# Decoder layer in one kernel: the inversion stages begin one slot later and stand closer, the second low-rank product two slots later, the second solve in a slot of its own

## The chip, the cores and the metric

The kernel runs on one core of a Trainium2 chip. The metric is the device time of one execution in microseconds, taken as the median of three runs. The core's engines run in parallel and each takes its own instructions strictly in the order in which they were written: TensorE (PE, with its weight loads PEld) multiplies matrices, VectorE (DVE), ScalarE (ACT) and GpSimd (POOL) work element by element, SyncE (SP) issues the transfers. They wait for each other only through semaphores.

## The reference

One inference step of a decoder layer for 256 prompt rows and 8 sequences of 4 sample rows (NT = 288 columns in the kernel, NX = 296 with the 8 rows before the samples), model width 2048. Cut to what matters:

```
P  = rmsnorm(x) @ w_in                      # 2048 x 14784, the columns of all branches
r, k, v = shifted mixes of P's columns      # z = prw + mu * (prw_prev - prw)
w  = -softplus(-(w0 + tanh(wd) @ w2)) - 0.5 # first low-rank product;  decay = exp(-exp(w))
a  = sigmoid(a0 + ad @ a2)                  # second low-rank product
kk = k * k_kk;  kk = kk * rsqrt(sum(kk * kk over the head))
k  = k * (1 + (a - 1) * k_a)
per head of 64, over the rows in order:
    sa = S @ -kk;  S = S * w + sa x (kk * a) + v x k;  y = S @ r
h  = RG-LRU scan of the causal conv of P's columns (a second branch)
x  = x + (g_a * (h * gelu) @ w_rg_o + g_b * out(y) @ w_rw_o) @ w_o
x  = x + relu(rmsnorm(x) @ w_up)^2 @ w_down
x  = x + sigmoid(rmsnorm(x) @ w_ple_gate) * (p @ w_ple)
```

## The kernel before

All large products are done in units: one unit multiplies 128 columns of a weight matrix (2048 x 128, 1 MB, loaded by SP into `raw`) with the activations. ACT copies `raw` to `wh` (the rounded high part) and DVE forms `wl = raw - wh`; PE then does 3 x 16 matmuls per unit (`xh,wh`, `xl,wh`, `xh,wl`, `unit_part`, all recorded on line 612). There are two `wh`/`wl` buffers and two output banks, so one unit is prepared while the other is multiplied.

The first half of the kernel is a loop over 16 pairs of heads (`step`, passes it = 0 to 15 and a last step with it = 16). Each pass has six units (k, r, v, RG input, RG gate, merge gate), and each unit is cut into 8 parts of 6 matmuls: these are the 48 slots of a pass. After the unit's part in a slot, each of the engines does what two tables written by hand name for that slot:

- `LATE[slot]`: stages of the chain of the pair before (it - 1). The recurrence is done in chunks of 64 rows. For it, triangular matrices are inverted in five levels: `invert1a` to `invert5b`. In `inverta` PE multiplies `am` with `tt` and ACT copies the result to `yy` (two copies, lines 1107 and 1108); in `invertb` PE multiplies `yy` and `tn` both ways and DVE adds the result to `inv` (`tt` and `tn` are its two halves). Then for each chunk c: `r`c (PE, ACT copies to `rs`), `u`c, the solve (PE, DVE copies to `us`), `my`c (PE; DVE forms the next state `mp`).
- `EARLY[slot]`: stages of this pair. `wd`: ACT squares `zk` (the mixed k) to `ksq`, PE multiplies `w2s` with `low`, ACT takes the sigmoid of the result to `sigw`. `ad`: PE multiplies `a2s` with `low` into the same bank, once `sigw` has been read out (`sig_ready`); ACT takes the sigmoid to `siga`, DVE forms `kp`. `kk_sum`: PE sums `ksq` over the head, DVE takes it up as `rn`. `decay`: ACT takes an exponential of `sigw` and a root of `rn`, with a table load before each. `kk`: DVE's reciprocal.

Pass 0 has no LATE stages, the last step (units of the second merge gate) has no EARLY ones. Within a slot each engine's order is fixed. ACT: at the first slot of a unit the eviction of the unit before (`evict`, `gb_evict`), then, at parts 0 and 2 of a unit (`HI_AT`), half of the next unit's `wh` (`hi_half`, L1176), then the LATE stages, then the EARLY ones. DVE: at a unit's first slot the mix of the evicted k, r or v (`shift_mix`; `zk` at slot 8), at parts 3 and 4 (`LO_AT`) half of `wl` (L1658), then LATE, then EARLY. PE: the 6 matmuls, LATE, EARLY.

The first slots of a pass hold for DVE the end of the chain before (`var`, slot 46), `ar`, `bonus`, `rg_decay` and the masks of `pairwise` (slot 5: `both`, `inv`), and then `zk`.

Of the kernel before, what the change touches and what calls it, by code (L numbers as in the profile page):

```python
# [65 lines left out]
def constants():  # L66
# [48 lines left out]
HI_AT, LO_AT = (0, 2), (3, 4)  # L115
EARLY = {
    9: ["wd"],
    10: ["ad"],
    13: ["kk_sum"],
    15: ["decay"],  # L120
    18: ["kk"],
    22: ["cum"],
# [6 lines left out]
    4: ["rg_decay"],  # L129
    5: ["pairwise"],  # L130
    6: ["rg_root"],
    9: ["invert1a"],
    10: ["invert1b", "rg_scan"],
    11: ["state_in"],
    12: ["invert2a"],
    14: ["invert2b"],
    15: ["samp_pair"],
    16: ["invert3a"],
    18: ["invert3b"],
    21: ["samp_inv_a", "invert4a", "samp_inv_b"],  # L140
    22: ["invert4b"],
# [3 lines left out]
    28: ["samp_out", "r0"],  # L145
    30: ["u0"],
    31: ["my0"],
    34: ["r1", "u1"],
    36: ["my1"],
    37: ["r2"],  # L150
    39: ["u2"],
# [1746 lines left out]
```

## Time and profile before

| | |
|---|---|
| median of 3 runs | 2811.33 us (2808.49 to 2817.96) |
| the profiled execution: its own time | 2813.93 us |
| its span | 2812.2 us |
| PE busy | 2698.8 us, 96% |
| DVE busy | 1665.3 us, 59% |
| ACT busy | 1162.7 us, 41% |
| PE's mean granted clock | 0.976 of full |

The page sums busy times over the whole span. The loop over the pairs takes the time up to about 1465 us; behind it come the products without a chain beside them. "Idle" in brackets behind a row is the time that its engine stood still just before it, with what ended it.

### The profile page before, as it was taken

How to read it: one execution, taken by the hardware profiler on the slowest of the kernel's cores; microseconds unless marked ns; L12 is line 12 of the kernel's file. 1: busy time of each engine (PE TensorE's matmuls, PEld its weight loads, DVE VectorE, ACT ScalarE, POOL GpSimd, SP SyncE). 2: the span in 40 equal slices, each digit the busy share in tenths (PEclk: the TensorE clock that was granted, in tenths of full speed). 3: DMA queues.
4: the chain of work that ended last, by engine and by line, in shares of the span. 5: the costliest groups of instructions: out<-in, count | busy, mean ns of one | idle time of the engine just before them, and what ended most of it. 6: DMA issues, size and time to landing. Idle time of an engine off the chain costs nothing.

```text
span 2812.2 us, 57470 instructions
## 1 busy us (share of the span) xinstructions
PE 2698.8 (96%) x22780; PEld 2512.8 (89%) x22780; DVE 1665.3 (59%) x2962; ACT 1162.7 (41%) x1626; POOL 103.9 (4%) x89
## 2 busy tenths in 40 slices
PE   5999999999999999999999999999999999999997
PEld 5988888888888888888889999999999999999996
DVE  5666776666776656776644455655544544545655
ACT  3544455444455434454434333344433433423322
POOL 0000000000000000000000000000000000000000
PEclk8999999999999999999999999999999999999998
DMA  5533333333332333233346776555665565565653
GB/s 153 155 91 87 82 88 90 88 90 86 82 101 77 88 90 93 79 101 79 84 107 186 193 214 181 160 162 165 168 169 156 167 168 158 166 168 159 171 151 93
DMA packets 699658, 361.58 MB, mean 129 GB/s; under 512 B 43905, under 2 KB 698531, under 8 KB 698659
## 3 DMA queue, kind: packets, MB, share of 16 engines
q1 hardware_dynamic: 699598, 360.74, 47.2%
q8 instruction: 42, 0.69, 0.1%
q14 instruction: 18, 0.15, 0.0%
HBM read 346.12 MB, written 14.59 MB: 128 GB/s over the span
## 4 chain that ended last, share of the span: by engine, by line
PE 82%; DVE 10%; ACT 2%; issue 2%; DMA 2%; SPq 0%; DVEq 0%; ACTq 0%
PE bank L612 81%; DVE wl L1658 2%; DVE both L1319 1%; DVE sd L1646 1%; PE bank L640 1%; DVE yc L1322 1%; ACT L1064 1%; DVE ysq L1319 1%; DMA raw<-w_in 1%; DVE wl L1316 0%; DVE inv L1319 0%; DVE nrm L1322 0%; DVE sd L1319 0%; DVE sd L1325 0%; DVE ar L1322 0%
## 5 line engine op out<-in xcount | busy, mean ns | idle before, releaser
L612 PE MATMUL bank<-xh,wh 128*128 128x288 f32 (+1 forms) x3136 | 1012.3, 323 | 16.8 <-DVE xl L1319 9.7
L612 PE MATMUL bank<-xl,wh 128*128 128x288 f32 (+1 forms) x3136 | 941.9, 300 | 0.0
L612 PE MATMUL bank<-xh,wl 128*128 128x288 f32 (+1 forms) x3136 | 940.7, 300 | 0.0
L612 PEld LDWEIGHTS bank<-xh,wh 128*128 128x128 f32 x3136 | 601.7, 192 | 56.0 <-issue 14.2
L612 PEld LDWEIGHTS bank<-xl,wh 128*128 128x128 f32 x3136 | 603.9, 193 | 6.8
L1316 DVE TENSOR_TENSOR wl<-raw,wh 128x2048 fp32r<-128x2048 f32 x206 | 472.1, 2292 | 232.2 <-ACT wh L1008 232.1
L612 PEld LDWEIGHTS bank<-xh,wl 128*128 128x128 f32 x3136 | 603.5, 192 | 0.0
L612 PE MATMUL bank<-sbl,wh 128*128 128x288 f32 x1792 | 535.1, 299 | 0.0
L612 PE MATMUL bank<-sbh,wl 128*128 128x288 f32 x1792 | 532.9, 297 | 0.0
L612 PE MATMUL bank<-sbh,wh 128*128 128x288 f32 x1792 | 529.7, 296 | 1.1 <-DVE wl L1316 1.0
L1008 ACT ACTIVATE wh<-raw 128x2048 fp32r<-128x2048 f32 x206 | 392.5, 1905 | 287.1 <-PE bank L612 272.6
L612 PEld LDWEIGHTS bank<-sbh,wh 128*128 128x128 f32 x1792 | 338.3, 189 | 1.6 <-issue 1.2
L612 PEld LDWEIGHTS bank<-sbl,wh 128*128 128x128 f32 x1792 | 336.9, 188 | 0.0
L612 PEld LDWEIGHTS bank<-sbh,wl 128*128 128x128 f32 x1792 | 336.6, 188 | 0.0
L1658 DVE TENSOR_TENSOR wl<-raw,wh 128x1024 fp32r<-128x1024 f32 x204 | 245.0, 1236 | 5.7 <-ACT wh L1176 4.2
L1176 ACT ACTIVATE wh<-raw 128x1024 fp32r<-128x1024 f32 x204 | 212.5, 1051 | 64.2 <-PE bank L612 63.0
L1625 DVE COPY us<-bank 64x128 f32<-64x128 f32 x64 | 18.5, 289 | 225.2 <-PE bank L612 225.2
L1319 DVE TENSOR_TENSOR inv<-inv,bank 64x512 f32<-64x512 f32 (+1 forms) x160 | 100.8, 630 | 69.4 <-PE bank L612 61.0
L1319 DVE TENSOR_TENSOR rga<-rga,bank 128x288 f32 (+1 forms) x80 | 36.3, 454 | 149.5 <-PE bank L612 149.5
L1271 ACT ACTIVATE tmp<-tmp 128x288 f32<-128x288 f32 x64 | 28.5, 445 | 225.3 <-DVE tmp L1322 225.3
L1131 ACT ACTIVATE rs<-bank 64x128 f32<-64x128 f32 x64 | 17.5, 274 | 175.4 <-PE bank L612 175.4
L612 PE MATMUL bank<-inv,both 64*64 64x64 f32 x1280 | 54.5, 224 | 22.2 <-DVE inv L1319 22.2
(286 smaller groups left out, 2769.2 us busy)
## 6 DMA issues: line engine op xcount, KB each, us to landing
raw<-w_in SPq DMA_DIRECT2D x116, 1024.0 KB, 5.8
raw<-w_up SPq DMA_DIRECT2D x64, 1024.0 KB, 6.3
raw<-w_down SPq DMA_DIRECT2D x64, 1024.0 KB, 5.8
raw<-w_rg_o SPq DMA_DIRECT2D x16, 1024.0 KB, 5.9
raw<-w_rw_o SPq DMA_DIRECT2D x16, 1024.0 KB, 5.9
raw<-w_o SPq DMA_DIRECT2D x16, 1024.0 KB, 5.8
raw<-w_ple_gate SPq DMA_DIRECT2D x16, 1024.0 KB, 6.0
s<-state_rwkv SPq DMA_DIRECT2D x32, 128.0 KB, 3.8
```

Of the source, the lines that this page charges most:

```text
L612: return pe.matmul(out, lhsT, rhs, start=start, stop=stop, skip_group_check=True)
L640: return pe.transpose(out, in_, ident)
L1008: act.activation(wh[slot][:], raw[slot][:], ACT.Copy).then_inc(hi_done, 1)
L1064: act.activation(sigw[:], bank[7][:, 0:NT], ACT.Sigmoid, bias=ptu[:, W0:W0 + 1]).then_inc(sig_ready, 1)
L1176: act.activation(wh[slot][:, k, :], raw[slot][:, k, :], ACT.Copy).then_inc((half_done, hi_done)[part], 1)
L1271: act.activation(tmp[u][:], tmp[u][:], ACT.Square).then_inc(h_sq, 1)
L1316: dve.tensor_tensor(wl[slot][:], raw[slot][:], wh[slot][:].bitcast(F32), ALU.subtract).then_inc(lo_done, 1)
L1319: return dve.tensor_tensor(out, x, y, op)
L1322: return dve.scalar_tensor_tensor(out, x, s, y, op0, op1)
L1625: dve.tensor_copy(us[rc, :], bank[5][rc, 0:P]).then_inc(u_read, 1)
L1646: dve.reciprocal(sd[:], sd[:]).then_inc(ch.sem, ch.one())
L1658: ins = dve.tensor_tensor(wl[slot][:, k, :], raw[slot][:, k, :], wh[slot][:, k, :].bitcast(F32), ALU.subtract)
```

## The change

Only the two tables change. `ad` moves from slot 10 to 12 and `kk_sum` from 13 to 14. The inversion's levels 1 to 3 move: 1a from 9 to 10, 1b from 10 to 11, 2a from 12 to 14, 2b from 14 to 15, 3a from 16 to 17 (3b stays at 18). `state_in` moves from 11 to 12, `samp_pair` from 15 to 16. The solve `u1` moves from slot 34, where it stands behind `r1`, to 35. `wd` stays at slot 9.

```diff
 EARLY = {
     9: ["wd"],
-    10: ["ad"],
-    13: ["kk_sum"],
+    12: ["ad"],
+    14: ["kk_sum"],
     15: ["decay"],
...
 LATE = {
...
-    9: ["invert1a"],
-    10: ["invert1b", "rg_scan"],
-    11: ["state_in"],
-    12: ["invert2a"],
-    14: ["invert2b"],
-    15: ["samp_pair"],
-    16: ["invert3a"],
+    10: ["invert1a", "rg_scan"],
+    11: ["invert1b"],
+    12: ["state_in"],
+    14: ["invert2a"],
+    15: ["invert2b"],
+    16: ["samp_pair"],
+    17: ["invert3a"],
     18: ["invert3b"],
...
-    34: ["r1", "u1"],
+    34: ["r1"],
+    35: ["u1"],
     36: ["my1"],
```

## Rows read from the trace of the kernel before

**Rows 1.** The page's parts 1 and 4: busy times, and the chain that ended last.

```profile
PE 2698.8 (96%) x22780; PEld 2512.8 (89%) x22780; DVE 1665.3 (59%) x2962; ACT 1162.7 (41%) x1626; POOL 103.9 (4%) x89
PE 82%; DVE 10%; ACT 2%; issue 2%; DMA 2%; SPq 0%; DVEq 0%; ACTq 0%
```

**Rows 2.** PE's waits, whole span: releaser, total us, times, longest.

```profile
PE bank L612 <- DVE inv L1319: 22.2, 15, 1.5
PE bank L612 <- ACT sigw L1064: 17.8, 15, 1.2
...
PE bank L612 <- ACT rs L1131: 7.1, 16, 0.5
```

**Rows 3.** Timeline of PE, slots 9 to 11 of pass 13: start, duration.

```profile
1140.26 0.68 PE L612 MATMUL bank<-inv,both 64*64 64x64 f32 x16 [1.48 <-DVE inv L1319]
1140.87 0.75 PE L612 MATMUL bank<-low,w2s 96*128 96x288 f32 x2
1141.24 0.51 PE L612 MATMUL bank<-xh,wh 128*128 128x296 f32 x1
...
1142.36 0.68 PE L612 MATMUL bank<-yy,inv 64*64 64x64 f32 x16
...
1144.74 0.75 PE L612 MATMUL bank<-low,a2s 96*128 96x288 f32 x2 [1.23 <-ACT sigw L1064]
```

**Rows 4.** Timeline of ACT in the same slots.

```profile
1140.98 0.38 ACT L1107 ACTIVATE yy<-bank 64x256 f32<-64x256 f32 x1 [1.67 <-PE bank L612]
1141.37 0.38 ACT L1108 ACTIVATE yy<-bank 64x256 f32<-64x256 f32 x1
1142.33 0.54 ACT L1062 ACTIVATE ksq<-zk,ptu 128x288 f32<-128x288 f32 x1 [0.59 <-DVE zk L1322]
1142.89 1.28 ACT L1064 ACT_TABLE_LOAD   x1
1144.18 0.50 ACT L1064 ACTIVATE sigw<-bank,ptu 128x288 f32<-128x288 f32 x1
1144.58 1.05 ACT L1176 ACTIVATE wh<-raw 128x1024 fp32r<-128x1024 f32 x1
```

**Rows 5.** Timeline of DVE in the same slots.

```profile
1140.04 1.21 DVE L1319 TENSOR_TENSOR both<-ab,cst 128x1024 f32<-128x1024 f32 x1
...
1141.78 0.52 DVE L1322 SCALAR_TENSOR_TENSOR zk<-sd,ptu,ex 128x288 f32<-128x288 f32 x1
```

**Rows 6.** Timeline of PE, slots 34 to 36 and 42 to 43 of that pass.

```profile
1189.48 0.41 PE L612 MATMUL bank<-rs,inv 64*64 64x64 f32 x4 [0.45 <-ACT rs L1131]
1189.83 0.40 PE L612 MATMUL bank<-xh,wh 128*128 128x288 f32 x1
...
1191.61 0.37 PE L612 MATMUL bank<-us,tmb 64*128 64x128 f32 x1
...
1202.34 0.40 PE L612 MATMUL bank<-xh,wh 128*128 128x288 f32 x1
...
1203.34 0.37 PE L612 MATMUL bank<-us,tmb 64*128 64x128 f32 x1
```

**Rows 7.** Windows: stretch, length, busy us of each engine, PEclk (granted clock).

```profile
1045.22:1126.56 81.34, 77.85 (x775) 67.46 (x774) 57.05 (x134) 39.29 (x70) 6.41 (x5) 1.00 0.35 90
1126.56:1210.83 84.27, 80.76 (x776) 69.53 (x774) 57.04 (x134) 39.29 (x70) 6.40 (x5) 0.96 0.33 87
1176.60:1183.40 6.80, 6.80 (x33) 4.95 (x31) 0.00 (x0) 0.95 (x5) 0.00 (x0) 0.50 0.60 160
1395.10:1401.90 6.80, 6.00 (x50) 5.87 (x51) 3.61 (x12) 2.34 (x6) 0.00 (x0) 0.50 0.01 2
1410.80:1414.20 3.40, 0.88 (x29) 0.83 (x30) 0.00 (x0) 2.86 (x5) 0.00 (x0) 1.00 0.00 0
```

**Rows 8.** Timeline of PE, slots 10 and 18 of the last step.

```profile
1395.90 1.12 PE L612 MATMUL bank<-yy,inv 64*64 64x64 f32 x16 [3.08 <-ACT yy L1108]
...
1413.37 0.68 PE L612 MATMUL bank<-yy,inv 64*64 64x64 f32 x16 [2.52 <-ACT yy L1108]
```

## The prediction

> **What bounds the kernel.** I read the page first. PE is busy for 96% of the span and holds 82% of the chain that ended last [rows 1]: every us in which PE stands still or runs slowly is a us of the kernel, and time on DVE or ACT counts only where PE waits for it. Next, PE's waits [rows 2]. Three of them belong to the slots that the change touches. PE waits 15 times for `inv` (22.2 us), in front of `invert1a`: 1.48 us in each of passes 2 to 15 and 1.53 us in the last step, none in pass 1. It waits 15 times for `sigw` (17.8 us), in front of `ad`'s product: 1.23 us a pass, 0.67 in pass 1. And it waits 16 times for `rs` (7.1 us), in front of `u1`: 0.45 us a pass. That is the whole gain that could be had: 47 us, 3.2 us a pass.
>
> Then the timeline of one pass, engine by engine, to see what is late. DVE is behind when slot 9 comes: it has come through the masks of `pairwise`, ends the last of them at 1141.25, and only then mixes `zk`, done at 1142.30 [rows 5]. ACT needs `zk` for `ksq`, starts at 1142.33, and goes on through a table load (1.28 us), `sigw`, and the second half of `wh` [rows 4]. So in slots 9 and 10 ACT's queue hangs on DVE's `zk`, and what stands in it ahead of `ksq` gets done early, what stands behind it late. Before the change the two `yy` copies of `invert1a` stand ahead of `ksq`: done at 1141.75 [rows 4], and `invert1b` finds them ready at 1142.36 [rows 3].
>
> **The change, part by part.** No instruction is added or removed; the sum is of waits and of the clock.
>
> `invert1a` one slot later. PE has ended slot 9 at 1140.26 - 1.48 = 1138.78 [rows 3]. `wd`'s product takes it 0.37 us (1140.87 to 1141.24) and the six matmuls of a slot 1.12 us (1141.24 to 1142.36) [rows 3]. It would be at `invert1a` at 1140.27, just as `inv` is ready. The wait of 1.48 us goes.
>
> `ad` in slot 12. `sigw` is read at 1144.68 [rows 4], and in slot 12 PE comes far behind it. The wait of 1.23 us goes.
>
> `invert1b`: here the wait turns up again, larger. The copies of `invert1a` now stand at slot 10, and `wd` stays at slot 9. On ACT both `ksq` and `sigw` are therefore ahead of the copies, and so is the half of `wh` that ACT does at the start of slot 10. ACT's order becomes `ksq` (1142.33, still tied to `zk`: nothing in front of `zk` on DVE is moved), table load, `sigw`, `wh` until 1144.58 + 1.05 = 1145.63, and then the two copies. They begin 0.1 us before `wh`'s row ends, as `wh` did behind `sigw`, and take 1141.75 - 1140.98 = 0.77 us [rows 4]: `yy` is ready at 1146.30. PE comes to `invert1b` at 1140.27 + 0.61 (`invert1a`, 1140.26 to 1140.87 [rows 3]) + 1.00 (a slot, 1202.34 to 1203.34 [rows 6]) = 1141.88. Counted from the end of its last matmul it stands still some 4.4 us. New wait less old ones: 4.4 - 1.48 - 1.23 = +1.7 us a pass. `wd` and `ad` no longer share a group with an inversion stage but `ad` joins `state_in` and `kk_sum` joins `invert2a`: nine groups of small matmuls in slots 9 to 18 before and after, so no cost there.
>
> What is queued behind. On PE, everything: it is the bound. On DVE, `rg_scan` and half a `wl` now come ahead of `invert1b`'s addition; what hides them is the new wait itself: from `zk` at 1142.30 DVE has until PE has ended `invert1b`, at about 1147.5, 5.2 us. If they took longer, two slots and `state_in` still lie between `invert1b` and `invert2a`, some 3 us of cover. On ACT, `siga` comes after `state_in`'s copies, `decay` with its two table loads later than now, and the eviction of the second unit and `invert3a`'s copies after that. Adding up ACT's queue from 1146.3 on I get `yy` for `invert3b` within 0.1 us of PE's coming to it: no wait, with nothing to spare. If that cover is gone it costs tenths of a us a pass. `wl` of the next units is early enough (`hi_half` is at its place). SP and POOL have no stage in the tables; what SP waits for from the moved stages (`kk_mm` at slot 24, `state_mm` at slot 32) was done long ago in either order, so no transfer moves.
>
> `u1` in slot 35. The wait of 0.45 us goes, because PE does a slot meanwhile. But two slots in one piece take 1.78 us (1189.83 to 1191.61) and two with a group between them 2 x 1.00 [rows 6], so the split costs 0.22. Gain: 0.2 us a pass. DVE does the first half of `wl` in front of `us` now; it begins before PE gets to `u1` and takes 1.2 us, so `us` is there for `my1` a slot later. Bounds of this edit: -0.45 to +0.2.
>
> Together 1.7 - 0.2 = 1.5 us a pass with its clock at full; pass 1, where DVE has no chain behind it, has a new wait of some 2.3 us for its old 0.67, the same difference. 15 passes: +22 us. Pass 0 has no inversion. In the last step there is no `wd`; the copies are behind an eviction that waits for a transfer, and half a `wh` more comes ahead of them (+1.0 us), while PE has one slot more to do meanwhile: 0.
>
> The clock. PE's granted clock is at half (1.2 of 2.4 GHz) in some stretches, and a pass with none takes 81.34 us, one with 6.8 us at half 84.27 [rows 7]: 2.9 us for 6.8, 1.5 for 3.4. In the last step PE waited 1.53 us, did one slot and `invert1a`, waited 3.08 us [rows 8], and its clock was at half from 1395.1, 0.8 us before that wait ended, to 1401.9 [rows 7]. A wait of 2.52 us there left it at 1.00 [rows 7, 8], and so do the two waits of 1.48 and 1.23 in each pass now. The new wait of 4.4 us in one piece is longer than the one that was followed by half clock, so I take it that each of passes 2 to 15 gets such a stretch, beside the one after `samp_out` that it has already. Bounds: 0 if it does not come, 2.9 us for 6.8 in full. Some of it falls on the wait itself, where it costs nothing, and some passes will have 3.4 us only; by the last step (6.0 of 6.8 us not covered, 2.6 us) and a short one partly covered (1.0) I take 2.0 us, nearer to the one with its own row. 14 x 2.0 = +28 us.
>
> Sum: 22 + 28 = +50 us. The profiled execution took 2813.93 us for its span of 2812.2; with the change I expect a span of about 2862. The median of the runs shown is 2.6 us under the profiled execution's own time: 2811.3 + 50 = 2861.
>
> On table loads the Trainium skill ("ScalarE: Activation LUTs", section "What ACT_TABLE_LOAD costs") says that each switch costs the load and about 1.38 us of drain, 2.66 us in all. The trace does not agree: the load ends at 1144.17 and `sigw` starts at 1144.18, and `ksq` had ended 0.02 us before the load [rows 4]. If the drain were there the new wait would be 1.4 us longer, +21 us in 15 passes.
>
> **The rivals.** (a) The new wait comes, but no half clock with it: +22 us, 2833. For it: short waits leave the clock alone [rows 7]. Against it: 3.08 us did not. 12 in 100.
> (b) The new wait is met by slack that I do not see (a table load that ACT does ahead of `zk`, a DVE that gets to `zk` sooner): with the load of 1.28 us taken off, the wait is 3.1 us and the pass gains and loses about nothing, 2811 within 8 us. Against it: the load stands behind `ksq` in all passes. 5 in 100.
> (c) Faster: `yy` is ready when PE comes, and the waits just vanish. Then 2.7 + 0.2 us a pass, 15 passes, -43 us: 2768. The point that decides is `zk`: only were it done by about 1137.9 instead of 1142.3 would ACT be through with its four instructions and the copies by 1141.9, and `both` alone runs until 1141.25 [rows 5]. Rather, a part of it together with no half clock. 3 in 100.
> (d) More is lost: each stretch at half is 6.8 us or longer, or ACT's late `decay` makes a second wait at `invert3b`: +75 us or more, 2886. 8 in 100. The drain named above would give 2882; from the rows I give it 1 in 100 of these 8.
> (e) My forecast: both parts, 72 in 100.
>
> **How the numbers follow.** Forecast 2861. Below I take in (a), 2833, with room for a gain of `u1` in full (15 x 0.25 = 4 us); above, 14 stretches at 2.9 us (+13 us) and some tenths at `invert3b` (+5 us). Range 2829 to 2880. 0.3% (8 us) is about what a measurement of this kernel can tell from no change. Faster by more than that: (c) and a little of (b), 0.04. Within: 0.06. Slower: (a), (d), (e), 0.90.
>
> **What would show it.** In the new profile: no wait of PE for `inv` in passes 1 to 15, none for `sigw` or only the shortest, 15 waits for `yy` (L1108), some 4.4 us each, 60 to 65 us in all; `rs` waits gone but for tenths. ACT's order `ksq`, table load, `sigw`, `wh`, `yy`, `yy`. PEclk of a second half-clock stretch in each pass a few us after `invert1a`, the mean clock from 0.976 down to about 0.95. Passes 3 to 4 us longer than the 81.34 and 84.27 us of now. The prediction is wrong if `yy` comes before 1.6 us behind `sigw`'s row, if `zk` is earlier in the pass, or if a wait of over 4 us leaves the clock at full.

## The result and the profile after

The changed kernel takes 2884.50 us (median of five runs, 2879.75 to 2888.82) against 2811.33 for the kernel before (also of five, not three): 73 us slower, a ratio of 1.0258 with a 95% interval of 1.0245 to 1.0272. The forecast was 2861 with a range up to 2880: the side is right and so are two of its terms, but the loss is half as large again (73 us against 50), because a third term had been put at nothing. The profiled execution is the fastest of the five (2879.75 us, span 2878.0); its span is 65.8 us longer than before.

The page of the changed kernel, parts 1, 2 and 4:

```profile
PE 2743.5 (95%) x22780; PEld 2551.8 (89%) x22780; DVE 1667.9 (58%) x2962; ACT 1160.4 (40%) x1626; POOL 103.9 (4%) x89
PEclk8999999999989989999999999999999999999998
PE 82%; DVE 10%; ACT 3%; issue 2%; DMA 1%; DVEq 0%; SPq 0%; ACTq 0%
```

The same number of instructions, yet PE is busy 45 us longer than in [rows 1]: the same matmuls took longer, and that is the clock (its mean fell from 0.976 to 0.957). The other 21 us of the span are time in which PE stood still. Its waits, whole span:

```profile
PE bank L613 <- ACT yy L1109: 68.6, 16, 4.5
...
PE bank L613 <- ACT ysq L1140: 3.8, 16, 0.2
PE bank L613 <- DVE inv L1320: 3.1, 15, 0.6
```

Of [rows 2] the waits for `sigw` and `rs` are gone and that for `inv` is down from 22.2 to 3.1 us. In their place stands one for `yy`. It is 4.46 or 4.47 us in each of passes 2 to 15, 2.28 in pass 1, 3.80 in the last step. Pass 12, PE, the counterpart of [rows 3]:

```profile
1106.85 0.68 PE L613 MATMUL bank<-inv,both 64*64 64x64 f32 x16 [0.20 <-DVE inv L1320]
1107.46 0.41 PE L613 MATMUL bank<-xh,wh 128*128 128x296 f32 x1
...
1113.02 1.12 PE L613 MATMUL bank<-yy,inv 64*64 64x64 f32 x16 [4.46 <-ACT yy L1109]
```

ACT and DVE in the same slots, the counterparts of [rows 4] and [rows 5]:

```profile
1108.93 0.54 ACT L1063 ACTIVATE ksq<-zk,ptu 128x288 f32<-128x288 f32 x1 [3.03 <-DVE zk L1323]
1109.48 1.28 ACT L1065 ACT_TABLE_LOAD   x1
1110.78 0.50 ACT L1065 ACTIVATE sigw<-bank,ptu 128x288 f32<-128x288 f32 x1
1111.17 1.05 ACT L1177 ACTIVATE wh<-raw 128x1024 fp32r<-128x1024 f32 x1
1112.12 0.36 ACT L1108 ACTIVATE yy<-bank 64x256 f32<-64x256 f32 x1
1112.49 0.38 ACT L1109 ACTIVATE yy<-bank 64x256 f32<-64x256 f32 x1
```

```profile
1108.38 0.52 DVE L1323 SCALAR_TENSOR_TENSOR zk<-sd,ptu,ex 128x288 f32<-128x288 f32 x1
```

Read them together: PE had the first product of the inversion done by 1107.46, and ACT was idle for 3.03 us at that time. Yet it could not copy, because its next instruction in order was `ksq`, which waited for `zk`. Before, the copies stood ahead of `ksq` and filled that idle time.

Passes 2 to 15 as one window, before and then after (length, busy us of each engine, granted clock):

```profile
206.90:1377.98 1171.08, 1122.13 (x10825) 971.65 (x10824) 798.60 (x1863) 550.06 (x967) 89.61 (x70) 0.97 0.34 88
```

```profile
211.22:1446.57 1235.35, 1165.64 (x10825) 1009.86 (x10824) 800.84 (x1863) 547.98 (x967) 89.67 (x70) 0.92 0.32 83
```

64.3 us, 4.6 us a pass. In single passes and stretches of the changed kernel, the counterpart of [rows 7]:

```profile
1112.20:1118.80 6.60, 5.78 (x48) 5.53 (x49) 4.04 (x5) 0.95 (x4) 0.00 (x0) 0.50 0.00 0
1057.60:1071.00 13.40, 13.40 (x62) 11.42 (x60) 4.99 (x16) 2.95 (x7) 0.00 (x0) 0.50 0.21 54
1093.21:1180.42 87.21, 82.21 (x776) 71.38 (x774) 57.20 (x134) 39.13 (x70) 6.41 (x5) 0.94 0.32 85
1268.20:1359.40 91.20, 86.23 (x776) 74.67 (x774) 57.17 (x134) 39.11 (x70) 6.40 (x5) 0.89 0.31 81
```

The last number but two is the granted clock. The first row is the stretch at half clock that sets in during the new wait. The second lies within one behind `samp_out` that lasts 13.7 us; three of passes 2 to 15 have such a long one, before it was one of them. A pass takes 87 to 91 us instead of 81 to 84 (and once 87).

### The profile page after: what moved, and what is told of

It reads as the page before. It is cut to its first block, busy times and chain, and to the rows that moved or that the text cites. A ratio compares the mean times of both kernels' runs of the same rounds, so it can differ in the third digit from the quotient of the medians.

```text
span 2878.0 us, 57469 instructions
## 1 busy us (share of the span) xinstructions
PE 2743.5 (95%) x22780; PEld 2551.8 (89%) x22780; DVE 1667.9 (58%) x2962; ACT 1160.4 (40%) x1626; POOL 103.9 (4%) x89
## 4 chain that ended last, share of the span: by engine, by line
PE 82%; DVE 10%; ACT 3%; issue 2%; DMA 1%; DVEq 0%; SPq 0%; ACTq 0%
PE bank L613 81%; DVE wl L1659 1%; DVE both L1320 1%; PE bank L641 1%; DVE sd L1647 1%; DVE yc L1323 1%; ACT L1065 1%; DVE ysq L1320 1%; DMA raw<-w_in 1%; ACT wh L1177 1%; DVE wl L1317 0%; DVE inv L1320 0%; DVE nrm L1323 0%; DVE sd L1320 0%; DVE sd L1326 0%
## 5 line engine op out<-in xcount | busy, mean ns | idle before, releaser
L613 PE MATMUL bank<-xh,wh 128*128 128x288 f32 (+1 forms) x3136 | 1023.6, 326 | 17.6 <-DVE xl L1320 9.7
L613 PEld LDWEIGHTS bank<-xh,wh 128*128 128x128 f32 x3136 | 608.6, 194 | 61.7 <-issue 15.7
L613 PEld LDWEIGHTS bank<-xl,wh 128*128 128x128 f32 x3136 | 610.9, 195 | 6.9
L613 PEld LDWEIGHTS bank<-xh,wl 128*128 128x128 f32 x3136 | 610.1, 195 | 0.0
L613 PE MATMUL bank<-yy,inv 64*64 64x64 f32 x1280 | 61.0, 241 | 68.6 <-ACT yy L1109 68.6
L613 PEld LDWEIGHTS bank<-yy,inv 64*64 64x64 f32 x1280 | 49.8, 149 | 81.7 <-issue 73.2
```

The lines of the kernel that those rows point to most:

```text
L613: return pe.matmul(out, lhsT, rhs, start=start, stop=stop, skip_group_check=True)
```

## The experiments

Each was timed beside the kernel before, whose median was 2813.97 us beside e1 to e4, 2816.42 beside e5 to e8, 2815.06 beside e9 to e12. "Against before" below is the difference of these medians.

| run | median us | against before | ratio, 95% interval |
|---|---|---|---|
| changed kernel | 2884.50 | +73.2 | 1.0258 (1.0245 to 1.0272) |
| e1 wd behind 1a | 2776.74 | -37.2 | 0.9875 (0.9856 to 0.9893) |
| e2 1a back | 2772.49 | -41.5 | 0.9851 (0.9834 to 0.9867) |
| e3 filler | 2821.93 | +8.0 | 1.0026 (1.0013 to 1.0038) |
| e4 u1 alone | 2808.02 | -6.0 | 0.9978 (0.9962 to 0.9995) |
| e5 ad alone | 2796.59 | -19.8 | 0.9931 (0.9915 to 0.9948) |
| e6 scan at 12 | 2782.52 | -33.9 | 0.9892 (0.9873 to 0.9911) |
| e7 sample split | 2746.55 | -69.9 | 0.9758 (0.9742 to 0.9774) |
| e8 after, sample split | 2834.23 | +17.8 | 1.0071 (1.0054 to 1.0088) |
| e9 before, sample split | 2781.79 | -33.3 | 0.9882 (0.9863 to 0.9902) |
| e10 after, split, filler | 2807.29 | -7.8 | 0.9973 (0.9962 to 0.9984) |
| e11 1a back, split | 2759.54 | -55.5 | 0.9803 (0.9785 to 0.9821) |
| e12 wd, split | 2758.60 | -56.5 | 0.9801 (0.9783 to 0.9819) |

### Where the new wait comes from

**e1**, against the changed kernel:

```diff
-    9: ["wd"],
+    10: ["wd"],
```

> The changed tables, but wd at slot 10 instead of 9, so that ACT's two copies of invert1a stand ahead of ksq and sigw again. Theory A (the copies are late because they stand behind wd in ACT's queue): the wait of 4.46 us for yy goes, some 0.7 us for inv stays in front of invert1a, no second stretch at half clock. Against the kernel before: 1.48 + 1.23 - 0.66 + 0.3 (u1) = 2.35 us less in each of 15 passes, -35 us, about 2776. Rival B (the inversion stages standing closer together are what makes PE wait): the kernel stays at 2850 or more, with waits for yy or inv of over 2 us in front of later stages.

Measured: 2776.74 us, 108 us under the changed kernel, by one entry of a table moved by one slot. The waits of PE in these slots of a pass are two small ones:

```profile
704.98 0.68 PE L613 MATMUL bank<-inv,both 64*64 64x64 f32 x16 [0.65 <-DVE inv L1320]
...
713.19 0.68 PE L613 MATMUL bank<-inv,both 64*64 64x64 f32 x16 [0.92 <-issue]
```

The first was expected; the second, in front of `invert2a`, was not, and e6 takes it up.

**e2**, against the changed kernel:

```diff
-    10: ["invert1a", "rg_scan"],
+    9: ["invert1a"],
+    10: ["rg_scan"],
```

> The changed tables, but invert1a alone back at slot 9, ahead of wd. Theory A: the copies are early again, the wait for inv of 1.48 us is back, those for sigw and rs stay away: 1.23 + 0.3 us less than before in each of 15 passes, -23 us, about 2788. Rival B: as the changed kernel, 2850 or more, since 1b to 3a are as close together as there.

Measured: 2772.49 us, 16 us better than expected; the expectation had left the stretches at half clock as they were, and e11 takes that up. With e1 this settles the cause of the wait. In both, levels 1b to 3a, `ad` and `kk_sum` stand exactly as in the change, and both are 1.2 to 1.5% faster than the kernel before; what they share and the change lacks is that ACT's copies of `invert1a` come ahead of `ksq` and `sigw`. Rival B, the closer spacing, falls.

### What the parts are worth alone

**e4**, against the kernel before:

```diff
-    34: ["r1", "u1"],
+    34: ["r1"],
+    35: ["u1"],
```

> The kernel before with u1 at slot 35 alone. The wait for rs of 0.45 us goes, a group more costs 0.15 to 0.22: 0.3 us less in each of 16 passes, -5 us, 2806. Rival: the split costs as much as the wait, no difference; or DVE's half wl ahead of us makes my1 wait, +0.5 us a pass, 2819.

Measured: -6.0 us, as expected; the interval just excludes 1.

**e5**, against the kernel before:

```diff
-    10: ["ad"],
+    12: ["ad"],
```

> The kernel before with ad at slot 12 alone. Theory A: the wait for sigw (1.23 us a pass) goes, and ad joins invert2a, one group fewer in a pass (0.2 us): -18 to -21 us, about 2792. Rival: siga comes so late that kk_sum, one slot on, waits for it instead; then the wait has only moved, no difference.

Measured: -19.8 us, as expected. Two of the three kinds of edit are gains. What makes the change slow is `invert1a` past `wd`. How much of the two gains is the waits' and how much the clock's is not shown: the profiled executions of e4 and e5 have a mean clock of 0.979 and 0.978 against 0.976 before.

### What the clock makes of the wait

**e3**, against the changed kernel (`invert1b`, on PE; the products are not used):

```diff
+                    if name == "invert1b":
+                        for k in range(30):
+                            mm(bank[4][:, 0:NT], wh[1][:, 0, :], xh[:, 0, NB:NX], True, True)
                     l, part, count = int(name[6]), name[7], apart(one)
```

> The changed kernel with 30 more matmuls of 288 columns in front of invert1b in each pass, in the time in which PE waits for yy; their result is used by nothing. They take some 4 us, so the wait shrinks from 4.46 to under 1 us while PE gets to invert1b no earlier. Clock theory (the wait is followed by half clock, which costs 2.35 us a pass, and it moves the stretch after samp_out, 10 us in all): although PE has more to do, 30 to 45 us less than the changed kernel, about 2845, and one stretch at half clock a pass instead of two. Rival (the wait itself is all that is lost, the clock follows something else): the same time as the changed kernel or up to 5 us more, and the stretches stay.

Measured: 2821.93 us, 63 us under the changed kernel though PE has 480 matmuls more to do. The timeline of a pass:

```profile
729.40 4.16 PE L613 MATMUL bank<-xh,wh 128*128 128x288 f32 x30
734.04 0.27 PE L613 MATMUL bank<-yy,inv 64*64 64x64 f32 x2 [0.48 <-ACT yy L1112]
```

`invert1b` starts no earlier than in the changed kernel: 6.17 us from `invert1a` in both (1106.85 to 1113.02 there, 727.87 to 734.04 here). So not a microsecond of the lateness was mended; what changed is that PE worked in the meantime, and the stretch at half clock behind the wait is gone. The rival falls. The gain is larger than the 30 to 45 us expected, which points at the other stretch: in the profiled execution only 9 of passes 2 to 15 have half clock behind `samp_out`, where all 14 of the changed kernel's do.

**e8**, the changed kernel with `samp_out` in two parts (the same cut in e7, e9 to e12):

```diff
     28: ["samp_out", "r0"],
+    29: ["samp_out2"],
...
-                elif name == "samp_out":
-                    count = apart(one)
-                    pe.wait_ge(su_read, count)
+                elif name in ("samp_out", "samp_out2"):
+                    k_here = 0 if name == "samp_out" else 1
+                    if k_here == 0:
+                        count = apart(one)
+                        pe.wait_ge(su_read, count)
-                    for b in range(NB):
+                    for b in range(4 * k_here, 4 * k_here + 4):
                         mm(sample_out(b // 4)[:, b % 4, :], ms[:, b, :], dg[:, b, :], b % 4 == 0, False)
-                    for k in range(2):
+                    for k in (k_here,):
...
-                    done.then_inc(so_mm, 1)
+                    if k_here:
+                        done.then_inc(so_mm, 1)
...
-                elif name == "samp_out":
+                elif name == "samp_out2":
                     act.wait_ge(so_mm, one)
```

> The changed kernel with samp_out cut in two in the same way and nothing else. It keeps the wait of 4.46 us and the stretch at half clock behind it and takes away the other one, so what is left above the kernel before is the wait (+1.5 us a pass, 22) and its own stretch (2.35 us a pass, 33), less the some 35 us that the stretches after samp_out cost the kernel before: about 2835 to 2843. If both stretches are shown to be independent, half-clock time is some 7 us a pass. Rival (the stretch after samp_out is longer in the changed kernel because of the one before it, and goes on elsewhere): 2860 or more.

Measured: 2834.23 us, a little under the range of the clock theory (2835 to 2843) and far below the rival's 2860. Its passes are all alike, with the one stretch behind the wait:

```profile
717.23:802.56 85.33, 80.32 (x776) 69.67 (x775) 57.22 (x134) 39.30 (x70) 6.41 (x5) 0.96 0.33 86
```

**e9** is the kernel before with that cut alone. 

> The kernel before with samp_out cut in two, as in e7 and e8, and nothing else. Clock theory: the stretches at half clock after samp_out go, 23 x 3.4 us of them in its profile at 0.44 us lost per us, 35 us, against 0.14 us a pass for the group more: -33 us, about 2779, passes of 81.5 us all alike. Rival: the cut only moves the stretch, no difference or +2 us.

Measured: 2781.79 us, -33.3 us, as expected. **e10** is e8 with the filler of e3. 

> The changed kernel with samp_out cut in two and with the 30 unused matmuls of e3 in the wait for yy: neither stretch at half clock is left in a pass. What is left between it and e9 is the wait alone: 4.06 us more from invert1a to invert1b, 2.1 us less behind it, 0.3 for u1, so 1.65 us a pass, +25 us against e9, about 2804; against e8 30 us less, which is the price of the stretch behind the wait.

Measured: 2807.29 us; 25.5 us above e9 and 26.9 under e8 (25.6 by the differences to before), where 30 were expected. A pass of each, e9 first:

```profile
691.29:772.77 81.48, 77.99 (x775) 67.53 (x774) 57.05 (x134) 39.41 (x70) 6.41 (x5) 1.00 0.35 91
```

```profile
705.77:788.92 83.15, 82.13 (x805) 71.57 (x804) 57.22 (x134) 39.30 (x70) 6.41 (x5) 1.00 0.34 89
```

Both have the clock full (1.00), so their difference, 1.67 us, is the waits (with `u1`'s split), as the new kernel has them and the old one. Against e8's pass of 85.33 us, e10's is 2.18 us shorter: that is the price of the stretch behind the wait, 30.5 us in 14 passes. The median shows less because the filler is not free everywhere: in pass 1 the wait is 2.28 us and the filler some 4, and that pass takes 1.6 us longer in e10 than in e8.

e3 and e10 differ by the cut of `samp_out` alone, and by 15.8 us (8.0 and -7.8 against before). So what the cut takes away is 33.3 us in the kernel before, 55.4 in the changed kernel (e8), and only 15.8 once the filler has removed the stretch behind the wait. The two kinds of stretch are not independent: the first half of e8's rival, that the one behind `samp_out` is longer because of the one before it, fits this, though in e8 nothing goes on elsewhere.

### Tables compared, with and without the clock

**e6**, against e1:

```diff
-    10: ["invert1a", "rg_scan"],
+    10: ["invert1a"],
...
-    12: ["state_in"],
+    12: ["state_in", "rg_scan"],
```

> As e1_wd_behind_1a (changed tables, wd at slot 10), and rg_scan at slot 12 instead of 10. In e1's trace PE still waits 0.92 us a pass in front of invert2a; DVE has 3.2 us of rg_scan and half a wl in front of invert1b's addition there. Theory: that addition is the cause; the wait goes, -14 us against e1, about 2763. Rival: the wait is for the second half of wl or for am, then it stays and the time is e1's, 2777.

Measured: 2782.52 us, not 2763: no gain on e1. But the wait of 0.92 us is gone, so the theory about its cause holds and its price does not. The pass shows where it went, e1 first:

```profile
691.27:772.71 81.44, 79.52 (x776) 68.85 (x774) 57.06 (x134) 39.28 (x70) 6.40 (x5) 0.98 0.35 90
```

```profile
690.28:772.20 81.92, 80.92 (x775) 69.62 (x774) 57.05 (x134) 39.27 (x70) 6.40 (x5) 0.96 0.35 90
```

PE is 1.4 us longer busy with the same work, at a clock of 0.96 instead of 0.98: the stretch behind `samp_out` is 6.8 us in every pass of e6 from the fourth on, and in e1's 3.4 us in three passes out of four and none in the next.

**e12** and **e7** are e1 and e6 with `samp_out` cut. 

> As e1_wd_behind_1a with samp_out cut in two: e7 but for rg_scan, which is at slot 10 here and at 12 there. Theory: rg_scan's move does save the 0.92 us a pass in front of invert2a, and e6 lost it again to more time at half clock: here, with the clock full, 14 us above e7, 2760. Rival: the move saves nothing, 2746.

> As e6_scan_at_12, and samp_out cut in two by output bank, the second half one slot on, at slot 29, with ACT's copies behind it. PE's sparse small matmuls, some 4 us in one piece before, then have a slot of full matmuls between them. Clock theory: the stretch at half clock after samp_out goes (one of 3.4 us a pass in e1, 1.5 us each) against 0.2 us for a group more: -18 us against e6, about 2745. Rival: the stretch stays or comes later, then +3 us against e6.

Measured: 2758.60 and 2746.55 us. That e7 came out at its figure of 2745 is luck in part: the cut was given 18 us against e6 and took away 36, while e6 itself had come out 20 above its own figure. With the clock full, e12's pass first, the move of `rg_scan` shows its 1.0 us a pass:

```profile
684.19:764.28 80.09, 78.16 (x776) 67.58 (x774) 57.05 (x134) 39.41 (x70) 6.40 (x5) 1.00 0.35 91
```

```profile
677.55:756.63 79.08, 78.10 (x775) 67.56 (x774) 57.02 (x134) 39.39 (x70) 6.40 (x5) 1.00 0.36 93
```

**e11** is e2 with `samp_out` cut. 

> As e2_1a_back (changed tables, invert1a back at slot 9) with samp_out cut in two. With the clock out of the way the tables can be compared: e2 had one wait of 1.48 us for inv, e7's tables have one of 0.65. Expected 0.8 us a pass above e7 less e7's one group more (0.2): 2746 + 9 = 2755. Rival: same as e7.

Measured: 2759.54 us, 13 above e7, where 9 was expected: e2's good place without the cut was partly the clock's doing. e7 is the best version: 2.4% faster than the kernel before and 4.8% faster than the changed one.

## Why the prediction was right and wrong

**The loss, taken apart.** From e9 to e10 the waits, from e10 to e8 the stretch behind the wait, from e8 to the changed kernel the stretch behind `samp_out`, less what that costs the kernel before (to e9). The third column goes by the medians, as differences to the kernel before timed beside each; the last by the passes shown above, 14 times the difference of one (mean of the changed kernel 88.24, of the kernel before 83.65).

| term | forecast | whole kernel, medians | passes 2 to 15, profiled executions |
|---|---|---|---|
| new wait less old ones, `u1` | +22 | +25.5 (e10 - e9) | +23.4 (83.15 - 81.48) |
| half clock behind the new wait | +28 | +25.6 (e8 - e10) | +30.5 (85.33 - 83.15) |
| half clock behind `samp_out` | 0 | +22.1 (55.4, changed kernel - e8, less 33.3) | +10.4 (88.24 - 85.33, less 83.65 - 81.48) |
| sum | +50 | +73.2 | +64.3 |

The first two terms come out near the forecast in both columns. The third differs between them for two reasons. The intervals of the three runs in its median figure make some 8 us together. And the profiled execution of the changed kernel is the fastest of the five: its mean clock is 0.957, that of the others 0.952 to 0.955, so they had more time at half clock.

**Right: the old waits go.** `sigw` and `rs` are gone; `inv` in front of `invert1a` keeps 0.2 us instead of none, because PE got there 0.2 us sooner than I had added up.

**Right: the copies are late by ACT's order.** `yy` was computed as ready 4.0 us after `zk`'s end (1146.30 less 1142.30). In the trace it is 1112.87 less 1108.90, also 4.0. The wait was given as 4.4 us and is 4.46. e1 and e2 show that the order on ACT is the cause.

**Right: nothing behind it.** `invert3b` does not wait, and none of PE's other waits, on DVE's account or on a transfer, has grown by 1 us over the whole span. The split of `u1` gains 0.4 us a pass by e4's medians, where 0.2 was taken; e4's interval, 0.1 to 0.7, holds both.

**Right, on table loads.** `ksq` ends at 1109.47, the load runs from 1109.48 to 1110.76, `sigw` starts at 1110.78: nothing beside the 1.28 us, as before. By the Trainium skill ("ScalarE: Activation LUTs", section "What ACT_TABLE_LOAD costs") some 1.38 us of drain would be added; this trace does not show it, and the measurement decides.

**Right: half clock follows the wait.** It does in every one of passes 2 to 15. The price, given as 2.0 us a pass, is 2.2 by the passes of e8 and e10 (1.8 by the medians, 25.6 over 14). It was reached by a mixture that did not come: of the 14 stretches 13 last 6.8 us and one 3.4, where several short ones had been allowed for. This is of a kind with what the Trainium skill tells of idle gaps ("TensorE: Matmul & The Clock Gate", section "HAM oscillation — how this bites in real kernels"), where in one kernel every wait for a transfer is followed by matmuls at the slow clock; for the wait of 4.46 us the trace agrees, with 0.50 over 6.6 us. In pass 1, which the forecast left out, the length of the wait does not decide it: after the same wait of 2.28 us (ended at 144.95 and at 142.74) the changed kernel, first row, has half clock and e8, second row, has not.

```profile
146.20:149.60 3.40, 3.40 (x15) 3.34 (x16) 2.54 (x3) 0.13 (x1) 0.00 (x0) 0.50 0.00 0
```

```profile
143.40:146.80 3.40, 3.40 (x40) 3.23 (x35) 2.60 (x3) 0.99 (x3) 0.00 (x0) 1.00 0.00 0
```

**Wrong: the stretch behind `samp_out`.** The step that failed is the one that set the new stretch "beside the one after `samp_out` that it has already", and so held the latter at its old price, without a reason. I had the rows for its not being fixed: one pass of 81.34 us with none, one of 84.27 with 6.8 us [rows 7], with the same instructions. In the changed kernel it cost 55 us instead of 33 by the medians, and 10 us more than before in the passes of the profiled executions. That was outside the sum, and outside the range, whose upper end held only longer stretches behind the wait and tenths at `invert3b`. That the stretch varies, that it goes when `samp_out` is cut (e7 to e12), and that it costs less once the one behind the wait is gone (e3 against e10) is shown; by what rule its length comes out as none, 3.4, 6.8 or 13.7 us in a pass stays open.

**The rivals.** (a), the wait without the clock, would have been 2833: e10 is that case (cut and filler aside) and shows 25 us for the waits. (b) and (c) needed `yy` sooner. (d), more lost, came nearest in its figure, 2886, but that is luck: of its two ways, the wait at `invert3b` did not come, and the stretches behind the wait did last 6.8 us nearly all, but at 2.2 us each and not the 3.8 that +75 would need. The chances for slower, (a), (d) and (e), add up to 0.92 and not to the 0.90 that was written.

## What to carry to other kernels

Where engines work through queues in a fixed order, moving a stage moves it past others in every queue. Before `invert1a` went behind `wd`, the question was what ACT's next instruction waits for: here two copies of under 0.4 us each, behind a late operand and a table load, hold up the bounding engine by 4.5 us. And on an engine whose clock can fall, a tuning step of 1 us a pass should be compared with the clock full in both kernels: here the stretches at half clock hid a gain (e6) and made a loss three times what the waits account for. Cutting the sparse stage alone (e9, -33 us) gave about as much as all the moves of stages behind it (e9 to e7, -35 us), and made the passes equal.

## What was not expected of the hardware

The clock falls without idle time just before. In the kernel before, the profile has PE busy for the whole of the 3.5 us before a stretch at half clock began, with the small matmuls of `samp_out` (16 of 68 columns, then ones of 16 and 256 columns on 32 and 64 rows):

```profile
1173.10:1176.60 3.50, 3.50 (x30) 2.75 (x28) 3.36 (x9) 0.00 (x0) 0.00 (x0) 1.00 0.07 18
```

From 1176.6 on the clock is at 0.50 [rows 7]. With a slot of full matmuls between the two halves of the stage, none of passes 1 to 15 has such a stretch in e7 and e9; only the last step, with waits of its own, has half clock. And matmuls whose result nobody uses can be worth their time: 30 in each pass took 4.16 us in a wait and made the kernel 63 us faster.
